# One program part for both layers of a hybrid encoder: the memory norm of layer 1 inside the last output projection of layer 0

## What is computed

```python
for i in range(DEPTH):
    h = rmsnorm(x, pre_g[i])
    mem_n = rmsnorm(mem, mem_g[i])
    mixed = ssd_branch(h, mem_n, ...) if i % 2 == 0 else na_branch(h, mem_n, ...)
    x = x + rmsnorm(mixed @ w_out[i], post_g[i])

# ssd_branch, its end
y = (y_fwd + y_bwd + d_skip[:, None] * xs).reshape(b, t, BRANCH_WIDTH)
y = rmsnorm(y * jax.nn.silu(z[..., :BRANCH_WIDTH]), norm_g)
m = memory_attention(q_mem, mem_n, w_mem_kv) * jax.nn.silu(z[..., BRANCH_WIDTH:])
return jnp.concatenate([y, m.astype(y.dtype)], axis=-1)
```

## Time and profile before

| | us |
|---|---|
| median of 3 runs (2286.46, 2289.37, 2289.39) | 2289.37 |
| the profiled execution | 2283.41 |
| its span, first to last instruction | 2281.7 |
| TensorE busy | 2160.7 (95%) |
| VectorE busy | 1080.4 (47%) |
| ScalarE busy | 731.9 (32%) |
| GpSimd busy | 936.9 (41%) |

### The profile page before, as it was taken

How to read it: one execution, slowest core, us unless ns; L and a number is a source line. 1 busy time by engine, 2 the same in 40 slices (tenths; PEclk the granted TensorE clock), 3 DMA queues, 4 the chain that set the end, 5 groups by cost and what they waited for, 6 DMA issues and landing times.

```text
span 2281.7 us, 32088 instructions
## 1 busy us (share of the span) xinstructions
PE 2160.7 (95%) x13298; PEld 1859.5 (81%) x13298; DVE 1080.4 (47%) x1676; ACT 731.9 (32%) x1665; POOL 936.9 (41%) x624
## 2 busy tenths in 40 slices
PE   6989999899999999995999999999999999999997
PEld 5878887688888889875778887888888888888885
DVE  3104332587888888884730232243342333343235
ACT  4113122334353435342332222142423233242343
POOL 4533332242433433331653333554544444454444
PEclk9999999899999999997999999999999999999999
DMA  5221112243322322212641111232222212112211
GB/s 179 89 59 57 48 53 80 94 116 97 106 95 74 103 81 98 79 56 74 203 139 47 56 47 55 64 119 72 61 59 63 62 57 61 58 56 71 64 48 65
DMA packets 216332, 180.57 MB, mean 79 GB/s; under 512 B 23323, under 2 KB 188475, under 8 KB 216187
## 3 DMA queue, kind: packets, MB, share of 16 engines
q1 hardware_dynamic: 216187, 178.52, 25.1%
HBM read 168.71 MB, written 12.21 MB: 79 GB/s over the span
## 4 chain that ended last, share of the span: by engine, by line
PE 48%; DVE 3%; DMA 1%; issue 1%; ACT 1%; POOL 0%; POOLq 0%; SPq 0%; DVEq 0%
PE bank L214 29%; PE bank L261 7%; PE bank L896 2%; PE bank L2026 2%; PE bank L2041 2%; PE bank L2016 2%; PE bank L922 1%; PE bank L2003 1%; DMA R<-macc_dram 1%; PE bank L955 1%; DVE acc L820 0%; PE bank L2084 0%; DVE acc L816 0%; PE bank L420 0%; PE bank L950 0%
## 5 line engine op out<-in xcount | busy, mean ns | idle before, releaser
L214 PE MATMUL bank<-Hh,Wh 128*128 128x256 f32 (+1 forms) x2192 | 756.0, 345 | 21.0 <-POOL Wl L191 8.2
L188 POOL TENSOR_SCALAR Wh<-Wraw 128x1024 fp32r<-128x1024 f32 x217 | 255.8, 1179 | 1260.7 <-issue 824.8
L214 PE MATMUL bank<-Hl,Wh 128*128 128x256 f32 (+1 forms) x2192 | 741.3, 338 | 0.0
L214 PE MATMUL bank<-Hh,Wl 128*128 128x256 f32 (+1 forms) x2192 | 740.0, 338 | 0.0
L191 POOL TENSOR_TENSOR Wl<-Wraw,Wh 128x1024 fp32r<-128x1024 f32 x217 | 550.5, 2537 | 18.1
L214 PEld LDWEIGHTS bank<-Hh,Wh 128*128 128x128 f32 x2192 | 419.8, 192 | 72.1 <-issue 21.1
L214 PEld LDWEIGHTS bank<-Hh,Wl 128*128 128x128 f32 x2192 | 419.0, 191 | 44.0
L214 PEld LDWEIGHTS bank<-Hl,Wh 128*128 128x128 f32 x2192 | 420.0, 192 | 41.0 <-issue 1.9
L295 DVE TENSOR_TENSOR acc<-bank,acc 128x512 f32<-128x512 f32 x240 | 165.3, 691 | 177.9 <-PE bank L261 177.1
L261 PE MATMUL bank<-Wh,Mh 128*128 128x512 f32 x552 | 219.6, 398 | 19.8 <-DVE acc L295 9.3
L261 PE MATMUL bank<-Wh,Ml 128*128 128x512 f32 x552 | 216.7, 393 | 0.0
(11 more groups left out here) (216 smaller groups left out, 2712.2 us busy)
## 6 DMA issues: line engine op xcount, KB each, us to landing
Wraw<-in_na_w_in_dram SPq DMA_DIRECT2D x80, 512.0 KB, 3.7
Wraw<-in_ssd_w_in_dram SPq DMA_DIRECT2D x57, 512.0 KB, 4.0
Wraw<-in_w_out_dram SPq DMA_DIRECT2D x48, 512.0 KB, 3.5
R<-acs_dram SPq DMA_DIRECT2D x16, 1536.0 KB, 6.2
Wraw<-in_w_mem_kv_dram SPq DMA_DIRECT2D x32, 512.0 KB, 3.9
R<-gs_dram SPq DMA_DIRECT2D x32, 128.0 KB, 3.4
macc_dram<-acc SPq DMA_DIRECT2D x1, 3072.0 KB, 10.2
R<-macc_dram SPq DMA_DIRECT2D x6, 512.0 KB, 5.8
```

What stands on the lines that cost most here:

```text
L188: pool.tensor_scalar(Wh[:, s, :], Wraw[:, s, :], 1.0, 1.0, ALU.mult, ALU.mult).then_inc(pool_c, 1)
L214: mm = pe.matmul(DB[h.k % 2][:, 0:t1 - t0], w[:, k, :], x[:, k, t0:t1], start=(k == 0 and i == 0), stop=(k == KC - 1 and i == 2))
```

## The change

It makes one block of the whole program and rearranges its middle.

- **Pairs 12 and 13.** Their first half of columns is projected in n = 14 as before; the second half moves to n = 15: tiles 0 to 2 ahead of pair 15's y on TensorE, tiles 3 to 5 behind it. The units' order becomes z14, half 0, z15, half 1. In n = 14 each convolution tap on VectorE stands ahead of two evictions.
- **Pair 15.** Its transposes and the squares of pair 14 stand between the two spans of z, not ahead of them.
- **Pairs 14 and 15** get own buffers for their high and low parts, so ScalarE doesn't wait for earlier projections. ScalarE writes pair 15's high part ahead of its square.
- **Memory norm of layer 1.** SyncE loads the memory tiles and gain in iteration 15's tail, before the weights of the last projection. ScalarE's four sums and root stand behind its copies of pair 15's states. VectorE waits for that root, normalises memory tile 0, and then evicts tiles 0 to 2 of the postponed half. Memory tile 1 is normalised before the last projection's evictions. In the last projection each memory tile's transposes stand behind two output tiles; its banks are A[1] to A[3]. The squares of pair 15 stand behind its first two tiles.
- **Layer 1** loads partial sums, residual and post gain in the same order relative to the units, the post gain now after the last eviction. Buffers of both layers are placed by address so that they don't overlap while both are in use; the attention's residual lies in three pieces and is loaded by three DMAs.

```diff
@@ memory_phase, sync
                         if L == 1:
+                            sp.wait_ge(ssd.stored, 16)
                             for i in range(2):
                                 load_macc(i)
...
+                    if L == 1 and u == 3:
+                        OF["sp"].k += 8 * 2 * NT
+                        sp.wait_ge(out_added, OF["sp"].value + 2)
+                        sp.dma_start(post_gain, post_g[0:1, :].broadcast_to([P, D])).then_inc(post_gain_landed, 16)
@@ memory_phase, new helpers
+            def load_mem(sp, i):
+                src = (mem_prompt if i < 2 else mem_sample)[0, i % 2 * P:(i % 2 + 1) * P, :]
+                sp.dma_start(mem[i], src).then_inc(mem_landed[i // 2], 16)
...
+            def mem_sums(act):
+                mem_norm.act_sums(act, place(0, D), lambda i: act.wait_ge(mem_landed[i // 2], 32) if i % 2 == 0 else None)
+
+            def mem_roots(dve, c):
+                dve.wait_ge(gain_landed, 16)
+                mem_norm.dve_roots(dve, c)
@@ ssd_phase
+            def mix(n):
+                if n >= LAST - 1:
+                    return last_mix[0][n % 2], last_mix[1][n % 2]
+                return Mh[:, n % 2, :], Ml[:, n % 2, :]
@@ ssd_phase, sync
-                    if out_in(n):
+                    if out_in(n) and n < LAST - 1:
                         load_out(sp, 0, slice((n - 2) * P, n * P))
+                    elif n >= LAST - 1:
+                        load_unit(sp, w_out[0, 12 * P:14 * P, (n % 2) * 512:(n % 2 + 1) * 512]
+                                  .rearrange("(k p) c -> p k c", p=P), 2)
...
+                sp.wait_ge(silu_done, x_silu(LAST))
+                for i in range(3):
+                    nxt.load_mem(sp, i)
+                sp.wait_ge(gated, LAST)
+                sp.wait_ge(x_scaled, PAIRS)
+                nxt.load_mem(sp, 3)
+                sp.wait_ge(ab_exp, PAIRS)
+                sp.wait_ge(seg_ready, PAIRS)
+                nxt.load_mem_gain(sp)
                 load_out(sp, 0, slice(14 * P, 16 * P))
-                sp.wait_ge(expanded, 22 * 16)
@@ ssd_phase, scalar
+                    def square():
+                        act.activation(z, y, ACT.Square).then_inc(sq_done, 1)
+
+                    if n == LAST:
+                        act.wait_ge(ab_exp, PAIRS)
+                        nxt.mem_sums(act)
                     act.wait_ge(gated, n + 1)
-                    act.activation(z, y, ACT.Square).then_inc(sq_done, 1)
+                    if n < LAST:
+                        square()
...
+                    if n == LAST:
+                        square()
+                for i in range(2):
+                    nxt.mem_norm.act_turned(act, i)
+                act.wait_ge(reduced, 1)
+                act.activation(sd, ssum, ACT.Sqrt, scale=1.0 / INNER, bias=eps[:, 0:1]).then_inc(rooted, 1)
+                for i in range(2, 4):
+                    nxt.mem_norm.act_turned(act, i)
@@ ssd_phase, vector
+                    if n == LAST:
+                        nxt.mem_roots(dve, c)
+                        nxt.mem_norm.dve_normed(dve, 0)
+                        U["dve"].k = out_unit(n - 1) + 2
+                        dve_out_tiles(dve, 1, (0, 1, 2))
+                    elif n == LAST - 1:
+                        U["dve"].k = out_unit(n)
+                        dve.wait_ge(dense_free, evicted(dense))
+                        for i, tiles in enumerate(((0, 1), (2, 3), (4, 5), ())):
+                            tap(j, n + 1, i)
+                            dve_out_tiles(dve, 0, tiles)
...
+                U["dve"].k = out_unit(LAST - 1) + 2
+                dve_out_tiles(dve, 1, (3,))
                 dve.wait_ge(gated, PAIRS)
                 low_part(LAST)
+                dve_out_tiles(dve, 1, (4, 5))
+                nxt.mem_norm.dve_normed(dve, 1)
                 U["dve"].k = unit0 + unit_index(PAIRS)
-                dve_out(dve)
+                for half in range(2):
+                    for k in range(2):
+                        dve_out_tiles(dve, half, (2 * k, 2 * k + 1))
+                        dve.wait_ge(summed, 1)
+                        nxt.mem_norm.dve_low(dve, 2 * half + k)
+                        if half == 0:
+                            nxt.mem_norm.dve_normed(dve, 2 + k)
+                    dve_out_tiles(dve, half, (4, 5))
...
@@ ssd_phase, tensor
                     else:
-                        turn_x(n)
-                        squares(n - 1)
-                        pe_dense(pe)
+
+                        def between():
+                            turn_x(n)
+                            squares(n - 1)
+
+                        pe_dense(pe, between=between)
...
-                    if out_in(n):
+                    if n == LAST:
+                        pe_out_tiles(pe, (0, 1, 2))
+                    elif n == LAST - 1:
+                        pe_mixed(pe)
+                        pe_out_tiles(pe, range(NT))
+                    elif out_in(n):
                         pe_out(pe)
...
-                pe_out(pe)
-
-                squares(LAST, summed)
-
+                pe_out_tiles(pe, (3, 4, 5))
+                pe_mixed(pe)
+                for half in range(2):
+                    for k in range(2):
+                        pe_out_tiles(pe, (2 * k, 2 * k + 1), last_mix)
+                        if half == k == 0:
+                            squares(LAST, summed)
+                        nxt.mem_norm.pe(pe, 2 * half + k)
+                    pe_out_tiles(pe, (4, 5), last_mix)
```

More of the change, by code:

```diff
@@ L246, in take_spans, with pe_out_tiles @@
                            lambda b: act.activation(dst[:, NP_:T], b[:, 0:NS], func, scale=scale)])
-        def pe_out_tiles(pe, tiles):
+        MIXED = ([Mh[:, k, :] for k in range(2)], [Ml[:, k, :] for k in range(2)])
+        def pe_out_tiles(pe, tiles, mix=MIXED):
+            hi, lo = mix
             u, o, od = U["pe"], OF["pe"], OD["pe"]
@@ L355, in encoder_kernel, with __init__ @@
         class Norm:
-            def __init__(self, name, tiles, gain, where, xn, small, H=None):
+            def __init__(self, name, tiles, gain, where, xn, small, H=None, banks=A[0:4]):
+                self.banks = banks
                 self.tiles, self.gain, self.where, self.xn, self.H = tiles, gain, where, xn, H or (Hh, Hl)
@@ L498, in memory_phase @@
             wkv = w_mem_kv[L]
[L499 to L509, removed]
-                pre.window(r)
[L511 to L521, removed]
+            if L == 0:
+                r = Region(phase, NR - 2 * KC * 512 - TAIL)
+                kT, vtok = r(8, 512), r(4, D)
+                v_at = [[vtok[:, t, 512 * i:512 * i + 512] for i in range(2)] for t in range(4)]
+                small = [r(10) for _ in range(3)]
+                nmax, psum_, pinv = r(NT), r(NT), r(NT)
+                pre.window(r)
+                xn = xx = [r(D), r(D)]
+                gain = r(D)
+                mem_all = r(4, D)
+                mem = [mem_all[:, i, :] for i in range(4)]
+            else:
+                kT = place(3072, 8, 512)
+                v_at = [[place(o, 512) for o in pair] for pair in
+                        ((1024, 1536), (12352, 13888), (14400, 14912), (7168, 7680))]
+                small = [place(8192 + 10 * i, 10) for i in range(3)]
+                nmax, psum_, pinv = (place(8222 + NT * i, NT) for i in range(3))
+                mem = [place(o, D) for o in (8240, 9264, 10288, 12864)]
+                gain, post_gain = place(2048, D), place(0, D)
+                xn, xx = [place(15488, D), place(3072, D)], [place(15488, D), place(11328, D)]
+                macc, res = mem[0:2], mem[2:4]
+                post = [place(15424 + NT * i, NT) for i in range(3)]
             with ExitStack() as kv_only:
@@ L871, in tensor @@
             def tensor(pe):
-                for i in range(4):
-                    mem_norm.pe(pe, i)
+                if L == 0:
+                    for i in range(4):
+                        mem_norm.pe(pe, i)
                 mem_norm.pe_end(pe)
@@ L1679, in attention_phase @@
                    (2, 128, 64, 2), (3, 0, 64, 4), (4, 128, 32, 8), (5, 0, 32, 7)]
[L1680 to L1683 removed]
+            mask = place(8240, NM)
+            gs, gq = place(15488, 2, 2, 256), place(11328, 2, 2, 192)
+            nmx, nmax, sums, rinv = (place(8064 + 2 * NT * i, NT, 2) for i in range(4))
+            ss, sd, rr = (place(8112 + NT * i, NT) for i in range(3))
             PT, Sb, Bm = heads(2, 12, P), heads(2, NSC), heads(2, NM)
[L1686 removed]
+            res_a, res_b, res_c = place(4992, 3, D), place(9200, 2, D), place(12096, 1, D)
+            res = [res_a[:, i, :] for i in range(3)] + [res_b[:, i, :] for i in range(2)] + [res_c[:, 0, :]]
+            gain, junk = place(13120, D), place(14144, D)
             (bm_ready, scored, max_ready, prob_ready, prob_normed, p_turned, pT_ready, pv_done,
```

207 lines of the change are left out of this document (112 added, 95 removed).

## The result

The changed kernel takes 2262.57 us (median of 4 runs, 2260.53 to 2263.44) against 2289.38 us; the ratio is 0.9883 with a 95% interval of 0.9866 to 0.9901, so 26.8 us or 1.2% faster. The forecast was 2262.4. The profiled execution took 2260.53 us.

A forecast was written before the change was run, and what follows sets the result against it. TensorE bounds the kernel nearly everywhere; the change rearranges only the seam between layers. Layer 1's first memory value unit, 1063.3 + 1.0 + 47.6 = 1111.9 against 1138.79, gains 26.9 us; 27 off 2289.37 gives 2262.4 us, range 2252 to 2273.

The forecast's parts named there:

- Half of pairs 12 and 13 leaves pair 14: Layer 0, pair 14: six output tiles instead of twelve put y of pair 14 7.9 us earlier, at 993.8.
- z of pair 15 isn't what pair 15 waits for: Pair 15: TensorE's 2.43 us wait goes, but VectorE and ScalarE set the pair; state copies end at 1017.2.
- The sums ahead of the evictions: Before pair 15's y: VectorE waits for the root, TensorE idles 12.6 us, y ends at 1034.1.
- Tiles behind y: Behind pair 15's y: three tiles fill TensorE's 5.17 us wait; the last projection starts 5.3 us after y.
- The last projection: Memory norm between its tiles: 16.4 + 1.2 + 3.3 + 3.0 us; layer 1's first memory key unit at 1063.3.
- the 3.0 us for VectorE's holding TensorE: In the last projection: VectorE's work holds TensorE now and then; 3.0 us added, bounds 1 and 8.
- Rival C: Last projection bound by VectorE: three normalised tiles at 3.3 us, 6 us more, gain 18 to 21; chance 0.20.
- From K to V: Layer 1's first memory key unit to first memory value unit: 1.0 + 47.6 us, set by VectorE's adding; ends 1111.9.
- All that follows V is untouched: Behind layer 1's first memory value unit nothing changes; the gain is how much earlier it starts, 26.9 us.
- B: Before pair 15's y: the root doesn't hold tile 2; y ends near 1028.5, gain 32.5 us (2257); chance 0.10.
- D: Seam through first key units: TensorE at its lower level, 0.44 for 0.23 us a matmul; slower, 2292; chance 0.02.
- E: Pair 15: memory loads so late that ScalarE's sums hold it, norm not moved in effect; 2286; chance 0.03.

The follow-up runs named there:

- e2: Changed kernel with pair 15's transposes and pair 14's squares put back ahead of z's first span; 2262.38 us.
- e1: Changed kernel with VectorE evicting tiles 0 to 2 of the postponed half ahead of the reciprocal and first normalised memory tile; 2259.09 us, ratio 0.9867 to the kernel before.
- e5: Changed kernel with ScalarE's evictions of the last two key units ahead of the last sum of squares of layer 0's result; 2256.36 us.
- e6: Changed kernel with the edits of e1 and e5 together; 2251.97 us.
- e7: Changed kernel with pairs 12 and 13 projected in one piece again, plus the early key unit evictions of e5; 2254.79 us.
- e9: The kernel of e8 measured once more, on the same chip as e7; 2250.05 us.
- e8: e6 with two tiles of the postponed half ahead of pair 15's y and four behind it, instead of three and three; 2250.79 us.

## Why the prediction was right, point by point

All from Z, where the prediction had Z at 984.91.

1. *Half of pairs 12 and 13 leaves pair 14.* y of pair 14 starts 8.77 us behind Z; forecast 8.9. Right.
2. *z of pair 15 isn't what pair 15 waits for.* Right, by e2, where tile 2 starts within 0.3 us of where it starts without that step. The copies of the states were to end at 1017.2, which is 32.3 from Z; they end at 1020.5, 31.9.
3. *The sums ahead of the evictions.* The root was forecast 38.8 from Z and ends at 38.1; TensorE's idle time was forecast as 12.6 and is 11.91; tile 2 41.0, measured 40.36; the end of y 49.2, measured 49.33 (47.72 in the second profile). e1 shows the cause. Tile 2 and y were put at 2.6 + 5.6 = 8.2 us and took 9.0 and 7.7 in the two profiles, so the close agreement with the first is in part luck. The root's table load took 1.28 us and the root started at once (1026.47), so the drain of 1.38 us that the Trainium skill (ScalarE: Activation LUTs, What ACT_TABLE_LOAD costs) adds isn't in this trace either.
4. *Tiles behind y.* The last projection starts 5.2 us behind y's end; forecast 5.3. Right.
5. *The last projection.* From y's end to K 29.2 were forecast, 27.9 measured. The mis-sized term is the 3.0 us for VectorE's holding TensorE: within the last projection it was 0.66. Against that the twelve tiles took 17.4 us in place of 16.4, 1.43 to 1.52 each where the steady tile has 1.36. The normalised tiles took 1.41, 1.27 and 1.28 us, not 3.3. GpSimd's splits of weights missed the last two. The first did run beside GpSimd (L188 and L191 are the two halves of a split), but started ahead of L191, and it was the split that took longer, 3.23 us where the next took 2.40:

```profile
1043.58 1.41 DVE L406 SCALAR_TENSOR_TENSOR R<-R 128x1024 f32<-128x1024 f32 x1
1044.01 3.23 POOL L191 TENSOR_TENSOR Wl<-Wraw,Wh 128x1024 fp32r<-128x1024 f32 x1
...
1049.92 1.27 DVE L406 SCALAR_TENSOR_TENSOR R<-R 128x1024 f32<-128x1024 f32 x1
...
1056.29 2.40 POOL L191 TENSOR_TENSOR Wl<-Wraw,Wh 128x1024 fp32r<-128x1024 f32 x1
...
1096.46 3.24 DVE L835 TENSOR_TENSOR acc<-acc,R 128x1024 f32<-128x1024 f32 x1
```

The last row, in the adding with GpSimd at work beside it (1.23 us without, at 1135.80 in the kernel before), shows that the price itself is real. Rival C asked for it in the wrong place, and took for granted that VectorE pays it whenever the two meet.

6. *From K to V.* 48.6 were forecast, 49.5 measured. VectorE's adding starts 1.0 us behind K, as forecast, and V comes 48.4 behind it. The term I had taken 1.0 off for freer DMA queues should have stayed at 48.6: the waits for partial sums did shrink, from 6.6 us in all to 4.0, but the first three additions took 7.05 us for 3. That the adding and not TensorE sets V is shown by e5. The prediction's "All that follows V is untouched" is not quite so: the longer wait in front of V (4.24 us for 1.97) makes the restart behind it slower, and at T the first profile has 26.4 us of its 27.2 left.

The two mis-sized stages nearly cancel (−1.3 and +0.9), and the second profile, with the same median, has 28.9 us from Z to V instead of 27.2: that 2262.4 meets 2262.57 is in part luck, that it lies near it is not. Of the rivals, B was not met as the change stands, but e1 has its mechanism: the hold removed, y ends 42.8 from Z where B had 43.6. C was not seen: TensorE idles 0.66 us between the last twelve tiles, where over 6 was its sign. Nor was D: every stretch of 10 us from 1040 to 1110 has the clock at 1.00. But the prediction's argument against D misreads its rows: the 5.3 us are only the tail at the first key unit. Before the change the clock was at 0.50 in both stretches of 10 us from 1070 to 1090, from the restart behind the longest wait on, with shorter waits in between. E is excluded by the loads: ScalarE's first sum starts with its copies' end.

Some of the prediction's sums are slightly off, none by enough to matter. VectorE's carries were put at 1019.4, where 1026.21 + 1.74 − 7.9 is 1020.05; they ended at 1019.1 on that scale. Twelve tiles at 1.36 are 16.3, not 16.4, and four groups at 0.8 are 3.2, not 3.3. D's 14.3 and 4.7 us stand for 72 and 24 matmuls slower by 0.21 us each, which is 15.1 and 5.0.

Not settled: e1 and e6 won 6.4 and 7.9 us of stage over their counterparts in the profiled executions (e1 4.8 against the second profile of the changed kernel) and 3.5 and 4.4 in the medians. Between e7 and e9 it is 8.6 us of stage at T against 4.7 in the medians. Part of it is y's length, which differs by 1.3 us between two executions of one kernel, and the restart at V, which differs by 0.8; whether the rest is chance ahead of Z these runs can't say. Nor does any run take out the own buffers or the single block.

## What to carry to other kernels

When work is drawn forward into the idle time of an engine, look where it stands on that engine's list relative to what frees another's buffers: here a normalised tile that wasn't transposed for another 19 us stood ahead of three evictions, and cost 5.5 us of TensorE's idle time. Put an eviction that another engine waits for ahead of what waits for a third engine; here two edits (e1 and e5) that move only an order, and no work, gave 10.6 us. And when a large part of a change shows no effect (the pieces: 0.6 us), take it out beside the suspected hold and again without it, before calling it worthless: the second time it was 4.7.

## What the runs showed of the hardware

Two executions of the same kernel, with the same idle time in front (11.91 and 11.92 us), gave the same 4.5 us of y at two lengths. The stretches around that wait in both (length; busy us of PE, PEld, DVE, ACT, POOL; granted clock; DMA share; GB/s), first the changed kernel:

```profile
1020.00:1030.00 10.00, 0.98 (x2) 0.83 (x3) 5.46 (x13) 6.59 (x13) 3.94 (x2) 0.58 0.22 68
1030.00:1040.00 10.00, 10.00 (x94) 8.60 (x93) 2.51 (x4) 0.00 (x0) 0.00 (x0) 0.74 0.01 2
```

and its second profile:

```profile
1020.00:1030.00 10.00, 1.21 (x6) 0.67 (x4) 5.64 (x11) 9.80 (x22) 3.90 (x2) 0.82 0.44 140
1030.00:1040.00 10.00, 6.87 (x74) 5.83 (x76) 3.35 (x5) 0.87 (x2) 0.00 (x0) 0.67 0.17 50
```

y took 6.11 us in the one and 4.85 in the other. Z lies 4.5 us later in the second, but in both the low level begins and ends within these 20 us (from 1010 to 1020 and from 1040 to 1050 the clock is 1.00). A mean of 0.58 over 10 us is 8.4 us at 1.2 GHz and the rest at 2.4; so the first had some 13.6 us at the low level, the second 10.2, for the same idle time. The low level went on for about 6 us behind the restart in the first (1029.02 to about 1035.2), for about 3.6 in the second. So a restart behind idle time has a price that varies by over 1 us from one execution to the next; a stage of one profile can't be trusted below that, and all that follows inherits it. The same shows behind the wait of 4.2 us at V (2.4 and 1.6 us, see e5) and in e8 and e9, whose y took 7.28 and 6.59 us behind 5.83 and 5.85 us of idle time. The other surprise is how far Z wanders: 9.7 us over twelve executions of work that is the same in all.
